# The MoE router reads transposes of the unnormalised residual; the row factor, the scale and the shift are moved out of its path

## Chip, cores and metric

The kernel runs on one core of a Trainium2 chip, in float32 throughout. The metric is the device time of one execution in microseconds (us); the changed kernel is compared with the kernel before on the same chip. Lower is better.

## What is computed

Two decoder layers over a batch of one with 512 tokens of width 1024. Layer 0 mixes tokens with differential attention, layer 1 with multi-head latent attention (MLA). After each mixer comes a hierarchical mixture of experts: a group (of 4) and then 2 of its 8 experts are chosen for each token. Cut to what the change touches, a layer ends like this:

```
x = x + g_m * mixer(...)                      # last product of the mixer: o @ w_o
h = rms_norm(x, norm_ffn) * (1 + sc_f) + sh_f # rows: 1/sqrt(mean(x^2)+eps); columns: gain, scale, shift
g_prob  = softmax(h @ w_group)                # 4 groups
e_logit = (h @ w_router) of the chosen group  # 4 x 8 experts
...top 2 experts, their weights..., w2(silu(h @ w1) * (h @ w3)) for each chosen expert
x = x + g_f * moe
```

The change rests on an identity: with r the row factor, g = norm_ffn * (1 + sc_f) and s = sh_f, `h @ W = r * (x @ (g * W)) + s @ W`.

## The kernel before

Tokens are cut into T = 4 tiles of 128 rows, channels into C = 8 chunks of 128. Every engine has its own instruction stream, written out by hand in the order in which it runs; semaphores (`sem("res")`, `sem("xt")`, ...) are the only ties between them. TensorE is `pe`, VectorE is `dve`, ScalarE is `act`, GpSimd is `pool`; `sp` issues nearly all weight loads. Since channels are laid out as `p*C + c`, a chunk c of a row is every eighth element of it.

The steps around the change, for layer l, with k = 2l + 1 (names, and lines in the profile):

- `project_out(l)` on TensorE: `product(t)` (L792, 32 records of 128x512 for a tile, two halves n of 16) multiplies the mixer's output by `w_o` into the two PSUM banks of tile t. In layer 0 `turn(t)` (L781) transposes the mixer's output first, and ScalarE's `output_turn` (L1343) copies it out.
- `residual(l, t)` on VectorE: for each half, times the gate row (L1761), then added to `X` (L1762). In layer 0 it also does the last conditioning dot products (L1587), which use up the semaphore `ada`.
- `squares` on ScalarE: sum of squares of the row (L1183), square root (L1185). `normalise_x` on VectorE: reciprocal (L1640), then row factor times `X`, read with stride 8 and written in chunk order to `XN` (L1641).
- `transpose_x` on TensorE (L620): 8 transposes of `XN`'s chunks, which read contiguous elements.
- `modulate` on ScalarE and VectorE, four chunks each (L1193, L1650): PSUM times scale plus shift, to `HT`.
- `logits(t)` on TensorE (L800, 16 records): `HT` times the router matrix `WGR`, 40 columns (32 experts and the 4 groups twice). `keep_busy(bank, n)` (L686) are n products (2n records) without use.
- `gate(l)` on VectorE: softmax, choice and ranks, starting with a maximum over all logits (L1817) and ending in `idx` (L1861). ScalarE does its exponential (L1450).
- GpSimd writes each `XN` tile to DRAM (`xn_d`, L2296) and each `X` tile (`kept_d`, L2297), in layer 0 then one more conditioning vector (`mod_d`, L2252, `gate_out`), whose landing it waits for. Then it gathers the rows of the first expert pairs from `xn_d` by `idx` (L2305).
- `experts(l)`: 16 steps, each with two experts (6 MB of weights). `turn_first_pair` (L874) transposes the first gathered rows; L884 and L899 are the products. SyncE loads expert weights (`expert_unit`, L518) into 20 slots; the slots from the fourth expert pair on are asked for only after both first gathers have landed, the two under `HT` after `sem("lg")`, those under `w_o` after the last `product`.

Of the kernel before, what the change touches and what calls it, by code (L numbers as in the profile page):

```python
# [26 lines left out]
ALU = mybir.AluOpType  # L27
# [3 lines left out]
P = 128  # L31
D = 1024
# [172 lines left out]
def build(nc, A, out):  # L205
    stack = ExitStack()
    with stack:
# [43 lines left out]
        CTL = sb("CTL", [1, 1 + TAILS], I32)  # L251
        posi = sb("posi", [P, T], I32)
# [352 lines left out]
        def _(pe):  # L605
# [7 lines left out]

            def transpose_x(k, t):

                if k in (1, 3):
                    pe.wait_ge(sem("res"), 4 * (k // 2) + t + 1)
# [153 lines left out]
            def project_out(l):  # L771
# [13 lines left out]
                def product(t):  # L785
# [4 lines left out]
                    for n in range(2):  # L790
# [6 lines left out]
                def logits(t):  # L797
                    modulated(k1, t)
                    for c in range(C):
                        last = mm(PB[0][:, t * NR:(t + 1) * NR], HT[:, c, t * P:(t + 1) * P], WGR[:, c, :],  # L800
                                  start=c == 0, stop=c == C - 1)
# [361 lines left out]
        def _(act):  # L1163
# [8 lines left out]
            fn(condb, condb, ACT.Silu).then_inc(sem("cond"), 1)  # L1172

            def squares(k, t):
# [10 lines left out]
                fn(sd[:, t:t + 1], ss[:, t:t + 1], ACT.Sqrt, bias=eps, scale=1.0 / D).then_inc(sem("sd"), 1)  # L1185
# [280 lines left out]
            def modulate_first_pair(l):  # L1466

                for h, (turned, done) in enumerate((("xh", "xhA"), ("xgt", "xA"))):
                    act.wait_ge(sem(turned), PAIRS * l + 1 if h else l + 1)
# [79 lines left out]
            output_root(3)  # L1549
            output_turn(2)  # L1550
# [6 lines left out]
            mla()  # L1557
            norm(3)
# [5 lines left out]
        def _(dve):  # L1564
# [49 lines left out]
            def first_block():  # L1614
# [5 lines left out]
                dve.wait_ge(sem("cond"), 1)  # L1620
# [16 lines left out]
            def normalise_x(k, t):  # L1637

                dve.wait_ge(sem("sd"), 4 * k + t + 1)
                link(v.reciprocal(rs[:, t:t + 1], sd[:, t:t + 1]))  # L1640
# [13 lines left out]
            def norm(k, update):  # L1654

                for t in range(T):
                    update((k - 1) // 2, t)
                    normalise_x(k, t)
                    if t:
                        modulate(k, t - 1)  # L1660
                modulate(k, T - 1)
# [90 lines left out]
            def residual(l, t):  # L1752
# [3 lines left out]
                for n in range(2):  # L1756
# [5 lines left out]
                    last = tt(X[:, t, cols], X[:, t, cols], tmp, ALU.add)  # L1762
                    if l == 0 and n == 0:
# [45 lines left out]
            def gate(l):  # L1809

                bgr = bgrs[:, l].rearrange("p (g e) -> p g e", g=NCOL)
                logits = PB[0][:, 0:T * NR].rearrange("p (t g e) -> p t g e", t=T, g=NCOL)
# [3 lines left out]
                dve.wait_ge(sem("lg"), 4 * (l + 1))  # L1816
                link(red(top, logits, AX.X, ALU.max))  # L1817
                tt(scores_, logits, over(top, 3, EPG), ALU.subtract).then_inc(sem("el"), 1)
# [27 lines left out]
                dve.wait_ge(sem("rank"), 2 * l + 1)  # L1846
# [8 lines left out]
                dve.wait_ge(sem("rank"), 2 * l + 2)  # L1855
# [88 lines left out]
            def modulate_first_pair(l):  # L1944

                for h, (turned, done) in enumerate((("xh", "xhD"), ("xgt", "xD"))):
                    dve.wait_ge(sem(turned), PAIRS * l + 1 if h else l + 1)
# [209 lines left out]
            def tables():  # L2157
# [14 lines left out]
                dve.wait_ge(sem("sin"), 1)  # L2172
# [5 lines left out]
                dve.wait_ge(sem("sin"), 2)  # L2178
# [23 lines left out]
            norm(1, residual)  # L2202
            gate(0)
            experts(0)
            gains(2)
            latents()
            mla()
            gains(3)
# [215 lines left out]
```

## Time and profile before

| | us |
|---|---|
| median of 3 runs (1142.84 to 1145.66) | 1144.5 |
| the profiled execution, its own time | 1146.95 |
| its span, first to last instruction | 1145.2 |
| TensorE busy, share of the span | 91% |
| VectorE busy | 53% |
| ScalarE busy | 29% |
| GpSimd busy | 8% |
| DMA, mean over the span | 298 GB/s |

The span is what the views of the trace speak of; 1.75 us of the profiled execution's time lie around it. Busy shares are means over the whole span: whether an engine matters in a stage is read in that stage.

### The profile page before, as it was taken

How to read it: one execution, taken by the hardware profiler on the slowest of the kernel's cores; microseconds unless marked ns; L12 is line 12 of the kernel's file. 1: busy time of each engine (PE TensorE's matmuls, PEld its weight loads, DVE VectorE, ACT ScalarE, POOL GpSimd, SP SyncE). 2: the span in 40 equal slices, each digit the busy share in tenths (PEclk: the TensorE clock that was granted, in tenths of full speed). 3: DMA queues.
4: the chain of work that ended last, by engine and by line, in shares of the span. 5: the costliest groups of instructions: out<-in, count | busy, mean ns of one | idle time of the engine just before them, and what ended most of it. 6: DMA issues, size and time to landing. Idle time of an engine off the chain costs nothing.

```text
span 1145.2 us, 15244 instructions
## 1 busy us (share of the span) xinstructions
PE 1043.2 (91%) x5634; PEld 629.8 (55%) x5634; DVE 608.7 (53%) x1464; ACT 328.3 (29%) x894; POOL 91.7 (8%) x129
## 2 busy tenths in 40 slices
PE   4999999999998999897879999899999999978996
PEld 3444444655566666554536555555457765655652
DVE  6899988895666422121246577677235622212224
ACT  4321122874221112120124554566112112111110
POOL 1000000000011221111000000000000111101100
PEclk9999999999999999999989999999998999999999
DMA  9929868309889999999996201300826799999998
GB/s 367 401 81 414 331 255 331 151 1 382 354 320 372 417 419 419 418 418 420 417 387 260 111 1 38 130 18 33 338 96 268 288 409 418 420 418 411 419 417 358
DMA packets 66814, 341.44 MB, mean 298 GB/s; under 512 B 11110, under 2 KB 11366, under 8 KB 36400
## 3 DMA queue, kind: packets, MB, share of 16 engines
q1 hardware_dynamic: 49952, 297.68, 64.3%
q0 software_dynamic: 15120, 37.63, 8.5%
q10 hardware_dynamic: 1664, 5.09, 1.1%
q8 instruction: 48, 0.79, 0.3%
q14 instruction: 30, 0.25, 0.1%
HBM read 320.90 MB, written 37.24 MB: 313 GB/s over the span
## 4 chain that ended last, share of the span: by engine, by line
PE 73%; DMA 11%; SPq 5%; DVE 5%; ACT 3%; issue 3%; DVEq 0%; ACTq 0%; POOLq 0%
PE PP L884 14%; PE PP L677 12%; PE PP L792 10%; PE PP L899 7%; SPq L518 5%; PE PP L699 3%; DMA AHS<-in_moe_w 3%; PE PP L1050 3%; DMA ring<-in_moe_w 3%; PE PP L1092 3%; PE PP L650 2%; DMA AHS<-y_d 2%; PE PP L1096 2%; PE PP L686 2%; PE PP L857 2%
## 5 line engine op out<-in xcount | busy, mean ns | idle before, releaser
L677 PE MATMUL PP<-ring,AHS 128*128 128x512 f32 x320 | 139.9, 592 | 0.0
L1957 DVE TENSOR_TENSOR PS<-PS,PP 128x256 f32<-128x256 f32 x33 | 13.9, 422 | 196.2 <-PE PP L884 186.6
L792 PE MATMUL PP<-ring,AHS 128*128 128x512 f32 x256 | 111.3, 593 | 1.4 <-ACT AHS L1421 0.8
L1964 DVE SCALAR_TENSOR_TENSOR PS<-PP,small,GF 128x512 f32<-128x512 f32 x66 | 46.5, 747 | 111.8 <-PE PP L899 101.5
L677 PEld LDWEIGHTS PP<-ring,AHS 128*128 128x128 f32 x320 | 59.7, 190 | 69.8 <-issue 69.8
L884 PE MATMUL PP<-RQK,RV 128*64 128x256 f32 x640 | 74.9, 392 | 11.5 <-issue 9.3
L792 PEld LDWEIGHTS PP<-ring,AHS 128*128 128x128 f32 x256 | 48.1, 190 | 59.7 <-issue 59.7
L884 PE MATMUL PP<-ring,RV 128*64 128x256 f32 (+1 forms) x608 | 75.5, 389 | 4.8 <-ACT RV L1455 1.7
L1479 ACT ACTIVATE PS<-PP 128x256 f32<-128x256 f32 x33 | 12.7, 384 | 219.0 <-PE PP L884 164.3
L884 PEld LDWEIGHTS PP<-RQK,RV 128*64 128x64 f32 x640 | 56.0, 141 | 33.3 <-issue 19.8
L884 PE MATMUL PP<-AHS,RV 128*64 128x256 f32 x640 | 71.8, 380 | 1.5 <-issue 1.5
L884 PEld LDWEIGHTS PP<-ring,RV 128*64 128x64 f32 (+1 forms) x608 | 55.6, 144 | 24.6 <-issue 9.0
L884 PEld LDWEIGHTS PP<-AHS,RV 128*64 128x64 f32 x640 | 53.5, 137 | 20.6 <-issue 6.3
L1703 DVE TENSOR_REDUCE small<-PP 128x2 f32<-128x256 f32 (+3 forms) x64 | 52.6, 823 | 16.4 <-PE PP L702 16.2
L2319 POOL DMA_INDIRECT y_d<-PS,row x31 | 31.6, 1020 | 342.5 <-DVE PS L1964 313.9
L1483 ACT ACTIVATE PS<-PP 128x256 f32<-128x256 f32 x33 | 12.7, 384 | 146.8 <-PE PP L891 146.8
L1587 DVE SCALAR_TENSOR_TENSOR ring<-ring,PS 128x1024 f32<-128x1024 f32 x44 | 51.9, 1221 | 3.5 <-DMA ring<-in_ada_t 3.1
L1933 DVE TENSOR_SCALAR RV<-PP,small 128x128 f32<-128x128 f32 x124 | 42.4, 406 | 18.2 <-PE PP L857 18.2
L1455 ACT ACTIVATE RV<-PP,small 128x128 f32<-128x128 f32 x124 | 46.6, 463 | 5.3 <-PE PP L857 5.3
L1281 ACT ACTIVATE AHS<-PP,small 128x512 f32<-128x512 f32 (+3 forms) x80 | 43.9, 558 | 14.3 <-DVE small L1703 14.1
L899 PE MATMUL PP<-AHS,PS 128*64 128x512 f32 (+1 forms) x168 | 40.2, 597 | 7.2 <-ACT PS L1483 6.5
L899 PE MATMUL PP<-ring,PS 128*64 128x512 f32 x160 | 36.5, 597 | 8.3 <-ACT PS L1483 5.4
(346 smaller groups left out, 1679.1 us busy)
## 6 DMA issues: line engine op xcount, KB each, us to landing
AHS<-in_moe_w SPq DMA_DIRECT2D x61, 1024.0 KB, 12.0
ring<-in_moe_w SPq DMA_DIRECT2D x58, 1024.0 KB, 19.1
RQK<-in_moe_w SPq DMA_DIRECT2D x52, 1024.0 KB, 20.4
ring<-in_ada_t SPq DMA_DIRECT2D x22, 1024.0 KB
AHS<-in_ada_t SPq DMA_DIRECT2D x18, 1024.0 KB
X<-in_moe_w SPq DMA_DIRECT2D x16, 1024.0 KB, 23.2
ring<-in_da_w_qkv SPq DMA_DIRECT2D x10, 1024.0 KB, 9.7
RQK<-in_ada_t SPq DMA_DIRECT2D x8, 1024.0 KB, 10.6
```

The costliest lines, as they stand in the source:

```text
L518: sp.dma_start(unit(slot), (w1, w3, w2)[k // 2][l][n + PAIRS * (k % 2)]).then_inc(s_w[slot], 16)
L677: last = mm(PB[qkv_bank(n)][:, :], HT[:, c, t * P:(t + 1) * P], us[c // 4][:, (c % 4) * NH:(c % 4 + 1) * NH], start=c == 0, stop=c == C - 1)
L699: mm(o[:, 0:L], mq[g // 2][0:QK, h, t * P:L], mk[g // 2][0:QK, h, 0:L], start=True, stop=False)
L792: last = mm(PB[2 * t + n][:, :], (OT, OTM)[l][:, k, t * P:(t + 1) * P], us[k // 2][:, (k % 2) * D + n * NH:(k % 2) * D + (n + 1) * NH], st ...
L884: last = mm(o[s0:s1, 0:FF], xgT[b][:, c, s0:s1], w(2 * m + e)[:, c * FF:(c + 1) * FF], start=c == 0, stop=c == C - 1)
L899: last = mm(PB[5 + m][s0:s1, :], hidT[:, c, s0:s1], w(4 + e)[:, c * D + m * NH:c * D + (m + 1) * NH], start=c == 0, stop=c == 1)
L1281: last = fn(dst[:, a, 0:L], PB[2 * pair + a][:, 0:L], ACT.Exp, bias=nmx[:, b, a:a + 1], accum_out=total)
L1455: last = fn(xgT[b][:, c, :], PB[0][:, (c // 2) * P:(c // 2 + 1) * P], ACT.Identity, bias=MODC[:, l, 3 + V_SHIFT, c:c + 1], scale=GC[:, 2 * ...
L1587: last = stt(wt, wt, 1.0, condb, ALU.mult, ALU.mult, accum_out=MODC[:, l, w, 2 * q + c:2 * q + c + 1])
L1703: red(nmx[:, b], PP[pair][:, :, 0:L], AX.X, ALU.max, negate=True).then_inc(sem("nm"), 1)
L1933: last = ts(xgT[b][:, c, :], PB[1][:, (c // 2) * P:(c // 2 + 1) * P], GC[:, 2 * l + 1, c:c + 1], MODC[:, l, 3 + V_SHIFT, c:c + 1], ALU.mul ...
L1964: last = stt(ysb[b][:, cols], PB[5 + m][:, :], weight, GF[:, cols], ALU.mult, ALU.mult)
```

## The change

In both layers TensorE transposes `X` itself, with stride 8, as soon as `residual` is done. What comes out of PSUM is copied without a factor: by ScalarE (chunks 0 to 3) and VectorE (chunks 4 to 7) for tiles 0 to 2, by VectorE alone for tile 3. GpSimd multiplies `WGR` once by the column scale. A product of the shift vector (broadcast) with `WGR`, before that multiplication, gives the same row in each partition, which ScalarE copies to `shifted`. The row factor is `exp(-0.5 ln(.))` on ScalarE instead of a square root and a reciprocal, and is applied to the logits together with `shifted` by `gate`. The normalised rows are still made for `xn_d`, the last tile's now by ScalarE. `product(3)` is cut into its two halves, with `transpose_raw(2)` and `logits(1)` between them and `logits(2)` behind. Compiled, ScalarE's stream has four table loads fewer. VectorE's `gains(3)`, one operation on 8 columns, stands ahead of layer 1's mixer instead of behind it.

```diff
+            def transpose_raw(k, t):
+                pe.wait_ge(sem("res"), 4 * (k // 2) + t + 1)
+                raw = X[:, t, :].rearrange("p (m c) -> p c m", c=C)
+                for c in range(C):
+                    last = nc.tensor.transpose(PB[2 * t + c // 4][:, c % 4 * P:(c % 4 + 1) * P], raw[:, c, :], ident[:, :])
+                    if t == T - 1 and c == C // 2 - 1:
+                        last.then_inc(sem("xh"), 1)
+                last.then_inc(sem("xt"), 1)
...
+                def router_shift():
+                    pe.wait_ge(sem("wgr"), 16 * (l + 1))
+                    pe.wait_ge(sem("gc"), k1 + 4)
+                    for c in range(C):
+                        last = mm(PB[4][:, 0:NR], MODC[:, l, 3 + V_SHIFT, c:c + 1].broadcast_to([P, P]), WGR[:, c, :],
+                                  start=c == 0, stop=c == C - 1)
+                    last.then_inc(sem("rank"), 1)
...
                 turn(1)
+                router_shift()
                 us = [take(l, "wo", u) for u in range(4)]
                 product(0)
+                if l == 0:
+                    pe.wait_ge(sem("wgs"), 2)
                 turn(2)
                 turn(3)
                 product(1)
-                transpose_x(k1, 0)
+                transpose_raw(k1, 0)
                 product(2)
-                transpose_x(k1, 1)
-                pe.wait_ge(sem("wgr"), 16 * (l + 1))
+                transpose_raw(k1, 1)
                 logits(0)
-                product(3)
-                transpose_x(k1, 2)
+                product(3, (0,))
+                transpose_raw(k1, 2)
                 logits(1)
-                keep_busy(3, 7)
-                transpose_x(k1, 3)
+                product(3, (1,))
                 logits(2)
+                keep_busy(3, 2)
+                transpose_raw(k1, 3)
                 logits(3)
...
     # ScalarE
-                fn(sd[:, t:t + 1], ss[:, t:t + 1], ACT.Sqrt, bias=eps, scale=1.0 / D).then_inc(sem("sd"), 1)
+                    chain.link(fn(sd[:, t:t + 1], ss[:, t:t + 1], ACT.Ln, bias=eps, scale=1.0 / D))
+                    fn(rs[:, t:t + 1], sd[:, t:t + 1], ACT.Exp, scale=-0.5).then_inc(sem("sd"), 1)
...
+            def raw_out(k, t):
+                act.wait_ge(sem("xt"), 4 * k + t)
+                fn(HT[:, 0:4, t * P:(t + 1) * P], PB[2 * t][:, :].rearrange("p (c q) -> p c q", c=4), ACT.Identity).then_inc(
+                    sem("hA"), 1)
...
                 squares(k, 0)
-                for t in range(T):
-                    if t + 1 < T:
-                        squares(k, t + 1)
-                    modulate(k, t)
+                squares(k, 1)
+                raw_out(k, 0)
+                squares(k, 2)
+                raw_out(k, 1)
+                raw_out(k, 2)
+                squares(k, 3)
+                act.wait_ge(sem("sd"), 4 * k + T)
+                fn(XN[:, 3, :].rearrange("p (c m) -> p c m", c=C), X[:, 3, :].rearrange("p (m c) -> p c m", c=C), ACT.Identity,
+                   scale=rs[:, 3:4]).then_inc(sem("xn"), 1)
...
     # VectorE
+                residual(l, 0)
+                normalise_x(k, 0)
+                residual(l, 1)
+                raw_out(k, 0, 1)
+                normalise_x(k, 1)
+                residual(l, 2)
+                raw_out(k, 1, 1)
+                normalise_x(k, 2)
+                residual(l, 3, lambda: raw_out(k, 2, 1))
+                raw_out(k, 3, 0)
+                raw_out(k, 3, 1)
...
-                dve.wait_ge(sem("lg"), 4 * (l + 1))
-                link(red(top, logits, AX.X, ALU.max))
+                for t in range(T):
+                    dve.wait_ge(sem("lg"), 4 * l + max(3, t + 1))
+                    last = stt(logits[:, t], PB[t // 3][:, t * NR:(t + 1) * NR], rs[:, t:t + 1], shifted[:, :], ALU.mult, ALU.add)
+                link(last)
+                link(red(top, scores_, AX.X, ALU.max))
...
     # GpSimd, ahead of its wait for the attention's end
+                pool.wait_ge(sem("rank"), 3 * l + 1)
+                g.tensor_tensor(WGR[:, :, :], WGR[:, :, :], GC[:, 2 * l + 1, :].unsqueeze(2).broadcast_to([P, C, NR]),
+                                ALU.mult).then_inc(sem("wgs"), 1)
```

Line numbers of the changed kernel differ: its L812 is the product's L792, L823 is L800, L695 is L686, L1825 and L1826 are L1761 and L1762, L1885 is the new operation of `gate`.

**TensorE, end of the output projection in layer 0**, before, from the second record of `product(3)` to the last logits:

```order
L792 MATMUL PP<-ring,AHS 128x512 x15
L620 MATMUL PP<-ident,RV 128x128 [waits s_xn,s_res]
L620 MATMUL PP<-ident,RV 128x128 x7
L800 MATMUL PP<-WGR,AHS 128x40 [waits s_hD,s_hA]
L800 MATMUL PP<-WGR,AHS 128x40 x7
L686 MATMUL PP<-ident 128x128 x7
L620 MATMUL PP<-ident,RV 128x128 [waits s_xn,s_res]
L620 MATMUL PP<-ident,RV 128x128 x7
L800 MATMUL PP<-WGR,AHS 128x40 [waits s_hD,s_hA]
L800 MATMUL PP<-WGR,AHS 128x40 x7
L800 MATMUL PP<-WGR,AHS 128x40 [waits s_hD,s_hA]
L800 MATMUL PP<-WGR,AHS 128x40 x7
```

and of the changed kernel, from the first logits behind the first half of `product(3)`:

```order
L823 MATMUL PP<-WGR,AHS 128x40 [waits s_hA]
L823 MATMUL PP<-WGR,AHS 128x40 x3
L823 MATMUL PP<-WGR,AHS 128x40 [waits s_hD]
L823 MATMUL PP<-WGR,AHS 128x40 x3
L812 MATMUL PP<-ring,AHS 128x512 [waits s_otev]
L812 MATMUL PP<-ring,AHS 128x512 x7
L823 MATMUL PP<-WGR,AHS 128x40 [waits s_hA]
L823 MATMUL PP<-WGR,AHS 128x40 x3
L823 MATMUL PP<-WGR,AHS 128x40 [waits s_hD]
L823 MATMUL PP<-WGR,AHS 128x40 x3
L695 MATMUL PP<-ident 128x128 x2
L620 MATMUL PP<-ident,X 128x128 [waits s_res]
```

The logits of tile 1 stand ahead of the last half product, those of tile 2 right behind it, and the last tile's transposes come after them and wait for `res`, no more for `xn`.

**VectorE, last half of tile 3 and start of `gate` in layer 0**, before:

```order
L1761 TENSOR_TENSOR PS<-PP,GM 128x512 [waits s_wo]
L1762 TENSOR_TENSOR X<-X,PS 128x512 [waits s_dve]
L1640 RECIPROCAL small<-small 128x1 [waits s_sd,s_res]
L1641 TENSOR_SCALAR RV<-X,small 128x1024 [waits s_dve]
L1650 TENSOR_SCALAR AHS<-PP,small 128x128 [waits s_xt,s_gc]
L1650 TENSOR_SCALAR AHS<-PP,small 128x128 x3
L1650 TENSOR_SCALAR AHS<-PP,small 128x128 [waits s_xt,s_gc]
L1650 TENSOR_SCALAR AHS<-PP,small 128x128 x3
L1817 TENSOR_REDUCE PS<-PP 128x20 [waits s_lg,s_iota,s_kept]
L1818 TENSOR_TENSOR PS<-PP,PS 128x160 [waits s_dve]
```

and of the changed kernel:

```order
L1825 TENSOR_TENSOR PS<-PP,GM 128x512 [waits s_wo]
L1826 TENSOR_TENSOR X<-X,PS 128x512 [waits s_dve]
L1709 COPY AHS<-PP 128x4x128 [waits s_xh,s_res]
L1709 COPY AHS<-PP 128x4x128 [waits s_xt]
L1885 SCALAR_TENSOR_TENSOR PS<-PP,small,shifted 128x40 [waits s_sd,s_lg,s_iota,s_kept]
L1885 SCALAR_TENSOR_TENSOR PS<-PP,small,shifted 128x40 [waits s_lg] x3
L1887 TENSOR_REDUCE PS<-PS 128x20 [waits s_dve]
L1888 TENSOR_TENSOR PS<-PS 128x160 [waits s_dve]
```

Reciprocal, normalisation and the eight scale-and-shift operations behind the last residual are gone; two copies of 128x512 and four small operations on the logits stand in their place.

**GpSimd, from the last tile's two writes to the first gathers in layer 0** of the changed kernel (before, the same rows stand there):

```order
L2369 DMA xn_d<-RV 128x1024 [waits s_xn]
L2370 DMA kept_d<-X 128x1024
L2322 DMA mod_d<-small 128x8 [waits s_mod]
L2378 DMA RV<-xn_d,idx 128x1024 [waits s_xd,s_idx,s_mo,s_res]
L2378 DMA RV<-xn_d,idx 128x1024
```

Nothing moved here; what `s_xn` waits for in the first row is now made by ScalarE, and the first gather waits, besides `idx`, for the landing of `mod_d` (`s_mo`).

## Rows read from the trace of the kernel before

**Rows 1.** Whole execution by core: span, granted clock
```profile
core 0: 1145.2 us, clock 0.984
```

**Rows 2.** Chain that ended last, in time: start us, us, what
```profile
349.75 5.91 DMA RV<-xn_d,idx
...
532.40 31.05 DMA AHS<-in_moe_w
...
1099.03 7.06 PE PP L884 x64
```

**Rows 3.** Timeline, layer 0 tail: start us, us, engine, line, operation [idle <-releaser]
```profile
328.69 1.04 PE L620 MATMUL PP<-ident,RV 128*128 128x128 f32 x8
...
328.89 0.69 DVE L1761 TENSOR_TENSOR PS<-PP,GM 128x512 f32<-128x512 f32 x1 [0.67 <-PE PP L792]
...
329.56 1.88 PE L800 MATMUL PP<-WGR,AHS 128*128 128x40 f32 x16
...
329.62 0.69 DVE L1762 TENSOR_TENSOR X<-X,PS 128x512 f32<-128x512 f32 x1
...
330.34 1.06 ACT L1183 ACTIVATE PS<-X 128x1024 f32<-128x1024 f32 x1 [13.53 <-DVE X L1762]
...
331.27 1.81 PE L686 MATMUL PP<-ident 128*128 128x128 f32 x14
...
331.52 0.30 ACT L1185 ACTIVATE small<-small 128x1 f32<-128x1 f32 x1
...
333.42 1.06 PE L620 MATMUL PP<-ident,RV 128*128 128x128 f32 x8 [0.35 <-DVE RV L1641]
...
334.59 1.50 ACT L1193 ACTIVATE AHS<-PP,small 128x128 f32<-128x128 f32 x4 [1.37 <-PE PP L620]
...
334.70 3.74 PE L800 MATMUL PP<-WGR,AHS 128*128 128x40 f32 x32 [0.21 <-DVE AHS L1650]
...
338.57 0.33 DVE L1817 TENSOR_REDUCE PS<-PP 128x20 f32<-128x160 f32 x1 [2.60 <-PE PP L800]
```

**Rows 4.** Timeline of the same steps in layer 1
```profile
867.47 1.04 PE L620 MATMUL PP<-ident,RV 128*128 128x128 f32 x8
...
873.47 4.54 PE L800 MATMUL PP<-WGR,AHS 128*128 128x40 f32 x32 [0.21 <-DVE AHS L1650]
...
878.15 0.33 DVE L1817 TENSOR_REDUCE PS<-PP 128x20 f32<-128x160 f32 x1 [3.41 <-PE PP L800]
```

**Rows 5.** Windows, one stretch of layer 1 (PEclk is third from the end)
```profile
873.00:878.00 5.00, 4.79 (x35) 4.44 (x33) 1.69 (x6) 2.79 (x5) 0.40 (x1) 0.82 1.00 371
```

**Rows 6.** Timeline where each output projection starts, both layers
```profile
265.91 1.91 PE L781 MATMUL PP<-ident,AHS 128*128 128x128 f32 x16
...
268.39 13.97 PE L792 MATMUL PP<-ring,AHS 128*128 128x512 f32 x32 [0.57 <-ACT AHS L1343]
...
805.77 2.38 PE L747 MATMUL PP<-AHS,RV 128*64 128x512 f32 x16 [0.83 <-ACT AHS L1297]
...
808.92 27.70 PE L792 MATMUL PP<-ring,AHS 128*128 128x512 f32 x64 [0.78 <-ACT AHS L1421]
```

**Rows 7.** Timeline, rows that price reads and copies
```profile
16.91 2.18 ACT L1225 ACTIVATE RV<-X,small 128x1024 f32<-128x1024 f32 x1 [3.27 <-DVE small L1623]
...
332.12 1.16 DVE L1641 TENSOR_SCALAR RV<-X,small 128x1024 f32<-128x1024 f32 x1
...
804.98 0.69 DVE L2135 COPY AHS<-PP 128x512 f32<-128x512 f32 x1 [1.25 <-PE PP L736]
```

**Rows 8.** Timeline, GpSimd's queue in layer 0
```profile
334.69 0.55 POOL L2252 DMA_DIRECT2D mod_d<-small  x1
...
349.75 1.10 POOL L2305 DMA_INDIRECT RV<-xn_d,idx  x1 [14.52 <-DVE idx L1861]
```

**Rows 9.** DMA issues, layer 0 stretch: KB each, us to landing
```profile
mod_d<-small POOLq DMA_DIRECT2D x1, 4.0 KB, 13.1
```

**Rows 10.** DMA issues, layer 1's first gather, us to landing
```profile
RV<-xn_d,idx POOLq DMA_INDIRECT x1, 4.2
```

More of the change, by code:

```diff
@@ L251, in build @@
         CTL = sb("CTL", [1, 1 + TAILS], I32)
+        shifted = sb("shifted", [P, NR])
         posi = sb("posi", [P, T], I32)
@@ L783, in turn, with product @@
                     last.then_inc(sem("ott"), 1)
-                def product(t):
+                def router_shift():
[5 more added lines that the diff above has]
+                    last.then_inc(sem("rank"), 1)
+                def product(t, halves=range(2)):
                     if l == 0:
@@ L789, in product @@
                         pe.wait_ge(sem("omla"), 8)
-                    for n in range(2):
+                    if t == 2:
+                        pe.wait_ge(sem("wgs"), 2 * (l + 1))
+                    for n in halves:
                         for k in range(C):
@@ L1199, in norm, with router_shift @@
                 squares(k, 0)
-                for t in range(T):
-                    if t + 1 < T:
-                        squares(k, t + 1)
-                    modulate(k, t)
+                squares(k, 1)
[7 more added lines that the diff above has]
+                   scale=rs[:, 3:4]).then_inc(sem("xn"), 1)
+            def router_shift(l):
+                act.wait_ge(sem("rank"), 3 * l + 1)
+                fn(shifted[:, :], PB[4][:, 0:NR], ACT.Identity).then_inc(sem("wgs"), 1)
             def root(out_, in_, scale, s):
@@ L1549, in _ @@
             output_root(3)
+            router_shift(0)
             output_turn(2)
@@ L1557, in _ @@
             mla()
+            router_shift(1)
             norm(3)
@@ L1652, in modulate, with raw_out, norm @@
                 last.then_inc(sem("hD"), 1)
[L1654 to L1661, printed above, removed]
+            def raw_out(k, t, half):
+                if half:
+                    dve.wait_ge(sem("xt"), 4 * k + t)
+                else:
+                    dve.wait_ge(sem("xh"), k)
+                v.tensor_copy(HT[:, 4 * half:4 * half + 4, t * P:(t + 1) * P],
+                              PB[2 * t + half][:, :].rearrange("p (c q) -> p c q", c=4)).then_inc(sem("hD" if half else "hA"), 1)
+            def norm(k):
+                l = k // 2
+                residual(l, 0)
[9 more added lines that the diff above has]
+                raw_out(k, 3, 1)
             def da_project():
@@ L1750, in output_norm, with residual @@
                     output_scaled(T - 1, half)
-            def residual(l, t):
+            def residual(l, t, between=lambda: None):
                 if l:
@@ L1762, in residual @@
                     last = tt(X[:, t, cols], X[:, t, cols], tmp, ALU.add)
+                    if n == 0:
+                        between()
                     if l == 0 and n == 0:
@@ L1811, in gate @@
                 bgr = bgrs[:, l].rearrange("p (g e) -> p g e", g=NCOL)
-                logits = PB[0][:, 0:T * NR].rearrange("p (t g e) -> p t g e", t=T, g=NCOL)
+                logits = scores_.rearrange("p t g e -> p t (g e)")
                 slots = picked.rearrange("p t k e -> p (t k) e")
@@ L1815, in gate @@
                 dve.wait_ge(sem("iota"), 2 * l + 1)
-                dve.wait_ge(sem("lg"), 4 * (l + 1))
-                link(red(top, logits, AX.X, ALU.max))
-                tt(scores_, logits, over(top, 3, EPG), ALU.subtract).then_inc(sem("el"), 1)
+                dve.wait_ge(sem("sd"), 4 * (2 * l + 1) + T)
+                for t in range(T):
[3 more added lines that the diff above has]
+                link(red(top, scores_, AX.X, ALU.max))
+                tt(scores_, scores_, over(top, 3, EPG), ALU.subtract).then_inc(sem("el"), 1)
                 dve.wait_ge(sem("ele"), l + 1)
@@ L2201, in _ @@
             dve.wait_ge(sem("gm"), 16)
-            norm(1, residual)
+            norm(1)
             gate(0)
@@ L2205, in _ @@
             gains(2)
+            gains(3)
             latents()
             mla()
-            gains(3)
             dve.wait_ge(sem("gm"), 32)
-            norm(3, residual)
+            norm(3)
             gate(1)
```

31 lines of the change are left out of this document (18 added, 13 removed).

## Prediction

> **What bounds the kernel now.** Start with the whole execution: one core, 1145.2 us of span, TensorE's granted clock at 0.984 [rows 1], so the clock is near its upper level but for short stretches. Then the chain that ended last, in order of time. Its long pieces are TensorE products and, in layer 0's experts, a weight load that TensorE waits 31 us of chain for; in layer 1's experts the pieces are TensorE products to the end (1099.03); in layer 0 the first gather (349.75, 5.91 us) links router and experts [rows 2]. Two consequences. In layer 0 the stream of expert weights decides the end, but it is resumed only when both first gathers have landed, so time gained or lost up to them is still passed on whole. In layer 1 the products decide, which start behind the same gather. I therefore read, in both layers, the stretch from the last product of the output projection to the gather.
>
> Let T0 be the moment at which TensorE starts what follows its last product half: 328.69 in layer 0, 867.47 in layer 1 [rows 3, 4]. The timeline behind it shows one long hand-over: residual to 330.31, squares, root, normalisation, transposes at 333.42, scaling, logits 334.70, and the router's first VectorE operation at 338.57. That is T0 + 9.88 in layer 0 [rows 3] and T0 + 10.68 in layer 1 [rows 4]; the 0.8 more is the logits' 32 records taking 4.54 instead of 3.74 us, in a stretch with a mean granted clock of 0.82, between the levels of 1.2 and 2.4 GHz [rows 5]. The operations from there to `idx` are the same before and after.
>
> **The change, part by part.** I first price everything as if a stride cost nothing.
>
> Ahead of T0, TensorE gets work. Sixteen logits records take 331.27 - 329.56 = 1.71 us, 0.107 each; eight transposes 0.87 [rows 3]. `router_shift` is 16 such records, 1.71. It partly fills idle time: in layer 0 sixteen transposes from 265.91 at 0.109 end at 267.65, and the first product starts at 268.39, so 0.74 is covered; in layer 1, 805.77 + 2.38 to 808.92 covers 0.77 [rows 6]. It costs 0.97 and 0.94. The transposes of tile 2 and the logits of tile 1 move from behind the last half product to ahead of it: 0.87 + 1.71 = 2.58. So T0 comes 3.55 and 3.52 later.
>
> Behind the new T0: logits of tile 2, 1.71; four `keep_busy` records at about 0.11, 0.45; transposes start at 2.16. `res` comes at 1.62 (329.62 + 0.69 - 328.69) and isn't waited for. Four transposes take 0.44. The first reader of eight transposes starts 1.17 after them, 0.30 beyond their 0.87 [rows 3]; so the first copy starts at 2.9. VectorE's PSUM copy of 128x512 takes 0.69 [rows 7]: 3.59, the second copy by 4.3. A signal costs 0.14 (end of the normalisation, 333.28, to 333.42). The first half of the logits runs 3.73 to 4.58, the second, no longer waiting, to 5.44. From the logits' last issue to VectorE it is 0.45 (334.70 + 32 x 0.107 to 338.57) [rows 3]: 5.9. The last of four 128x40 operations has no row; nothing bounds it below, the 0.33 of the 128x160 reduction above; I take 0.2 and get 6.1. The other three lie behind the logits. The tail is 3.8 shorter in layer 0 and 4.6 in layer 1. Net on `idx`: -0.2 and -1.1, the second mostly the clock, which may dip again.
>
> What costs nothing: ScalarE's and VectorE's copies for tiles 0 to 2, each with a product half of 6.9 us beside it; the table loads that are gone, which lay beside the residual's waits and the logits; GpSimd's 128x320 product, with product(0)'s 14 us before anyone waits for it. That last one stands ahead of GpSimd's zero fill of `y_d` in layer 0 and delays it, and the row writes behind it, by a few us; the gather that needs them leaves some 80 us later, at 349.75 [rows 8]. If this cover were gone, TensorE would wait for `wgs` ahead of `turn(2)`.
>
> **Stride.** The raw transposes read every eighth float, 32 bytes apart. No row shows TensorE doing so. Two other engines do, on the same `X`: ScalarE takes 2.18 us for 1024 elements [rows 7], against 1.06 for 1024 contiguous ones [rows 3], 2.06 times. VectorE takes 1.16 [rows 7], 0.145 per 128 elements with its fixed part. Bounds for one transpose: 0.109 (nothing), 0.145 (VectorE's pace), 0.22 (twice), 0.27 (ScalarE's pace). TensorE's present pace, 128 elements in 0.109, is 1.17 elements per ns, faster than ScalarE's contiguous pace of 0.97 and than VectorE's strided 0.88, so it is nearer to the engine that halves. I take 0.22, +0.11 each. Three tiles lie ahead of T0: 24 x 0.11 = 2.6. Behind it the first copy starts 0.44 later, the second waits for all eight (2.16 + 1.76 + 0.3 = 4.2, to 4.9), the second half of the logits starts at 5.03 instead of 4.58: +0.5. Together +3.1 per layer; `idx` moves by +2.9 and +2.0.
>
> The Trainium skill, "SBUF — State Buffer", section "Door 1: The DMA port swizzle", says that SBUF is read in lines of 16 bytes and that fp32 can be strided freely up to four elements; beyond that each access opens a new line and pays. By it stride 8 costs TensorE something and the sum is the +3.1 per layer; by VectorE's row, which shows hardly any price, it would be 28 x 0.036 = 1.0. ScalarE's 2.18 us agrees with the page, VectorE's 1.16 doesn't show it.
>
> **GpSimd's queue in layer 0.** The last tile's rows are now normalised by ScalarE: residual 1.62, squares to root 1.18 (330.34 to 331.52), logarithm and exponential at 0.30 each, like the root [rows 3], 2.18 for the strided read [rows 7], signals 0.2: ready at T0' + 5.8. Before, `mod_d` was issued at 334.69, 1.41 behind the end of the normalisation at 333.28, and took 13.1 us to land, at 347.8, behind 1 MB of rows and beside the weights [rows 8, 9]. GpSimd waits for it ahead of the first gather, which left at 349.75, released by `idx` [rows 8]: 2 us of margin. After, it is issued at T0' + 7.2, so at 328.69 + 3.55 + 7.2 = 339.4 without a stride price and 342.1 with it, and lands at 352.5 or 355.2. The gather then leaves 2.8 or 5.4 later than before, not with `idx`. In return fewer weights are beside it: layer 1's took 4.2 us [rows 10], layer 0's 5.91 [rows 2], so up to 1.7 comes back. Layer 0: between +2.9 (`idx` alone) and +5.4; I take +4. In layer 1 there is no `mod_d`; the writes of the rows have over 10 us.
>
> **Sum.** 4 + 2.0 = +6. The profiled execution would go from 1146.95 to 1153; it stands 2.45 above the median of the runs, 1144.5, so I forecast 1150.5.
>
> **Rivals.**
> - *The stride is free or nearly so for TensorE.* For it: VectorE's 1.16 us. Against it: ScalarE's row. Then `idx` comes 0.2 and 1.1 earlier; with `mod_d` late layer 0 gives +1 to +2.8: together about +0.7, 1145.2; with `mod_d` in time, -1.3, 1143.2. Not slower. It decides up to where 56 transposes' worth of extra cost makes 3.4 us with `mod_d` late: below 0.16 to 0.17 us a transpose.
> - *The stride costs, `mod_d` doesn't.* Its 13.1 us were spent beside the weight stream; issued later it may meet a shorter queue. Layer 0 then gives +2.9: total +4.9, 1149.4.
> - *TensorE reads at ScalarE's pace*, 0.27: another 0.05 x 28 x 2 = 2.8, 1153.
> - *Clearly faster.* Needs 3.4 us: the clock staying high through the router and the first products in both layers, beyond the 0.8 seen. Nothing in the rows gives as much; -4, 1140.5.
>
> **How the numbers follow.** 0.3% is about what a measurement of this kernel can tell from no change, 3.4 us. Stride doubled: 0.52, of which two thirds with `mod_d` late (the forecast), one third without. Nearly free: 0.36. ScalarE's pace or worse: 0.06. Clearly faster: 0.06. The doubled case's own range is 1148 to 1153; the free one's 1142.8 to 1146.5. Both together need 1143 to 1153.5. Slower: 0.52 x 0.9 + 0.06, with a little of the free case, 0.54; faster 0.06; same 0.40.
>
> **What would show it.** The pitch of the eight raw transposes (0.11 or 0.22) in the timeline; T0 at about 335 and 873.6; the router's first 128x160 reduction 6 to 7 us behind it; GpSimd's first gather in layer 0 released by the `mod_d` landing, later than 352; in layer 1 by `idx`. The prediction is wrong if the transposes keep 0.11, or if ScalarE's and VectorE's copies for tiles 0 to 2 make TensorE wait inside the projection.

## The result, and the profile after

The changed kernel took 1150.11 us (median of 7 runs, 1147.17 to 1152.87) where the kernel before took 1144.5 beside it (1142.78 to 1145.92): ratio 1.0038, 95% interval 1.0020 to 1.0056. A second set of runs, taken with the experiments, gave 1149.49 against 1146.54 over 35 runs of before, 1.0021 (1.0004 to 1.0038). These ratios are not the quotients of the medians, which are 1.0049 and 1.0026. So it is slower, by 2.4 to 4.4 us by the two ratios and by 3.0 to 5.6 us by the medians. The forecast was 1150.5.

The span answers to [rows 1]; this execution's own time was 1152.87, the longest of its seven.

```profile
core 0: 1151.0 us, clock 0.987
```

The timeline of layer 0 after the change, where the projection starts, answers to [rows 6]: start us, us, engine, line.

```profile
267.01 1.91 PE L790 MATMUL PP<-ident,AHS 128*128 128x128 f32 x16
...
268.76 1.88 PE L799 MATMUL PP<-WGR,small 128*128 128x40 f32 x16
...
270.46 1.96 PE L812 MATMUL PP<-ring,AHS 128*128 128x512 f32 x4
...
270.72 0.72 POOL L2352 TENSOR_TENSOR WGR<-WGR,small 128x320 f32<-128x320 f32 x1 [77.69 <-PE PP L799]
```

And its tail, which answers to [rows 3]:

```profile
333.46 1.88 PE L823 MATMUL PP<-WGR,AHS 128*128 128x40 f32 x16
...
334.38 0.69 DVE L1826 TENSOR_TENSOR X<-X,PS 128x512 f32<-128x512 f32 x1
...
335.69 1.04 PE L620 MATMUL PP<-ident,X 128*128 128x128 f32 x8
...
336.86 2.15 ACT L1243 ACTIVATE RV<-X,small 128x1024 f32<-128x1024 f32 x1
...
337.14 1.98 PE L823 MATMUL PP<-WGR,AHS 128*128 128x40 f32 x16 [0.41 <-DVE AHS L1709]
...
339.16 0.26 DVE L1885 SCALAR_TENSOR_TENSOR PS<-PP,small,shifted 128x40 f32<-128x40 f32 x1 [0.97 <-PE PP L823]
...
339.45 0.32 DVE L1887 TENSOR_REDUCE PS<-PS 128x20 f32<-128x160 f32 x1
```

Eight raw transposes take 1.04 us, as eight contiguous ones did [rows 3]. T0 is 333.46, and the reduction (339.45) stands 5.99 us behind it, where it stood 9.88 behind. GpSimd's queue in layer 0 answers to [rows 8, 9]; the last row is the view of DMA issues, with KB and us to landing.

```profile
340.41 0.55 POOL L2322 DMA_DIRECT2D mod_d<-small  x1
...
354.09 1.10 POOL L2378 DMA_INDIRECT RV<-xn_d,idx  x1 [13.13 <-DMA mod_d<-small]
...
mod_d<-small POOLq DMA_DIRECT2D x1, 4.0 KB, 12.8
```

`idx` was written at 349.49, so the gather waits 4 us for `mod_d` alone. Layer 1's tail answers to [rows 4]:

```profile
877.39 1.88 PE L823 MATMUL PP<-WGR,AHS 128*128 128x40 f32 x16
...
879.62 1.04 PE L620 MATMUL PP<-ident,X 128*128 128x128 f32 x8
...
883.38 0.32 DVE L1887 TENSOR_REDUCE PS<-PS 128x20 f32<-128x160 f32 x1
```

One pair of profiles is not enough to place a few us, so the table counts each stage from its own start, for all kernels timed here. A0 is the start of the 16 transposes of layer 0's attention output, A1 that of the 16 last value products of layer 1's attention, before as in [rows 6]; E is TensorE's first expert product, X the end of layer 0's last expert product, RQK SyncE's first load of expert weights into the buffer RQK. Each number is the difference of two starts in the timeline or the chain. The kernels below the changed one are those of the experiments.

| kernel | A0 | A0 to RQK | A0 to gather | A0 to E | A0 to X | X to A1 | A1 to gather | A1 to E | E to end |
|---|---|---|---|---|---|---|---|---|---|
| before | 265.9 | 62.20 | 83.84 | 91.55 | 301.3 | 238.6 | 83.48 | 91.06 | 248.4 |
| before_again | 266.5 | 62.20 | 84.70 | 91.40 | 301.4 | 241.8 | 83.47 | 89.58 | 250.0 |
| before_mod_late | 266.3 | 62.20 | 84.69 | 92.21 | 301.5 | 241.4 | 83.47 | 89.53 | 248.9 |
| before_early_ada | 265.5 | 56.91 | 83.81 | 91.25 | 300.2 | 240.3 | 82.60 | 90.18 | 248.8 |
| changed | 267.0 | 63.80 | 87.08 | 93.18 | 303.7 | 241.4 | 82.36 | 89.39 | 249.6 |
| after_again | 266.8 | 63.80 | 87.24 | 93.45 | 303.7 | 238.3 | 82.38 | 89.38 | 249.9 |
| mod_late | 266.9 | 63.80 | 83.52 | 92.82 | 302.5 | 238.4 | 82.37 | 89.35 | 249.7 |
| after_early_ada | 266.5 | 56.58 | 87.33 | 93.46 | 303.7 | 241.4 | 82.36 | 89.30 | 250.2 |
| two_gates | 265.9 | 56.57 | 83.54 | 92.00 | 300.7 | 237.0 | 82.35 | 89.93 | 248.1 |
| tail_order | 266.5 | 63.21 | 84.55 | 92.42 | 302.2 | 239.0 | 82.03 | 88.10 | 251.3 |
| both | 266.7 | 63.21 | 82.41 | 92.50 | 302.4 | 238.5 | 82.20 | 88.21 | 249.8 |
| all_three | 266.6 | 62.30 | 81.49 | 91.33 | 301.7 | 236.8 | 81.29 | 87.33 | 249.3 |
| all_four | 266.4 | 55.70 | 81.50 | 89.02 | 298.1 | 241.5 | 80.35 | 86.38 | 250.0 |

The end is that of the span. Three things are to be read here. X to A1, which the change hardly touches, varies from 236.8 to 241.8 in kernels of all kinds: of the 5.8 us between the two first spans, 2.8 are this, and no effect of the change. What the change does repeatedly is A0 to X, +2.3 us, and A1 to the gather, -1.1. The 1.1 us don't reach the experts: layer 1's first gather takes 5.2 us to land where it took 4.2 [rows 10], so it lands only 0.1 to 0.2 us earlier against A1 (87.5 to 87.6 in place of 87.7 to 87.8). From A1 to the end the first four kernels of the table need 338.4 to 339.6 us, the changed one 339.0 and 339.3. Here is the view of DMA issues, and the 5 us from just before this gather on (columns of the windows: GpSimd busy, PEclk, DMA share, GB/s), before and after:

```profile
RV<-xn_d,idx POOLq DMA_INDIRECT x1, 5.2
...
889.00:894.00 5.00, 2.08 (x2) 0.66 0.43 116
...
894.00:899.00 5.00, 2.08 (x2) 1.00 0.92 375
```

In the changed kernel the gather meets expert weights that are still under way: SyncE's loads behind the last product leave 3.7 us later against A1 (877.59 in place of 867.66). In tail_order and the kernels built on it the last product ends earlier again, and this gather lands 4.2 to 4.3 us after its issue.

### The profile page after: what moved, and what is told of

It reads as the page before. It is cut to its first block, busy times and chain, and to the rows that moved or that the text cites. A ratio compares the mean times of both kernels' runs of the same rounds, so it can differ in the third digit from the quotient of the medians.

```text
span 1151.0 us, 15203 instructions
## 1 busy us (share of the span) xinstructions
PE 1042.2 (91%) x5646; PEld 630.0 (55%) x5646; DVE 602.6 (52%) x1440; ACT 321.1 (28%) x876; POOL 93.7 (8%) x131
## 4 chain that ended last, share of the span: by engine, by line
PE 70%; DMA 14%; SPq 6%; DVE 4%; ACT 3%; issue 3%; POOL 0%; DVEq 0%; ACTq 0%; POOLq 0%
PE PP L910 13%; PE PP L686 12%; PE PP L812 10%; PE PP L925 7%; SPq L519 6%; DMA ring<-in_moe_w 5%; PE PP L708 3%; PE PP L1076 3%; DMA AHS<-in_moe_w 3%; PE PP L1118 3%; PE PP L659 2%; DMA AHS<-y_d 2%; PE PP L1122 2%; PE PP L745 2%; PE PP L756 2%
## 5 line engine op out<-in xcount | busy, mean ns | idle before, releaser
L686 PE MATMUL PP<-ring,AHS 128*128 128x512 f32 x320 | 139.9, 592 | 0.0
L812 PE MATMUL PP<-ring,AHS 128*128 128x512 f32 x256 | 111.8, 594 | 0.0
L686 PEld LDWEIGHTS PP<-ring,AHS 128*128 128x128 f32 x320 | 59.7, 190 | 69.8 <-issue 69.8
L812 PEld LDWEIGHTS PP<-ring,AHS 128*128 128x128 f32 x256 | 48.0, 190 | 56.9 <-issue 56.9
L1825 DVE TENSOR_TENSOR PS<-PP,GM 128x512 f32<-128x512 f32 x16 | 11.1, 692 | 65.0 <-PE PP L812 65.0
```

The lines of the kernel that those rows point to most:

```text
L686: last = mm(PB[qkv_bank(n)][:, :], HT[:, c, t * P:(t + 1) * P], us[c // 4][:, (c % 4) * NH:(c % 4 + 1) * NH], start=c == 0, stop=c == C - 1)
L812: last = mm(PB[2 * t + n][:, :], (OT, OTM)[l][:, k, t * P:(t + 1) * P], us[k // 2][:, (k % 2) * D + n * NH:(k % 2) * D + (n + 1) * NH], st ...
```

## Experiments

**after_again.** The changed kernel once more, beside the three edits that follow.

> The changed kernel, unchanged, timed again and profiled again. In the first trace the first gather of layer 0 leaves 4.3 us late, released by the landing of mod_d; between the layers another 2.5 us are lost in a stretch where four products take 3.6 instead of 1.9 us. Queue theory: the late gather is there again (GpSimd's first gather of layer 0 released by mod_d, 2.7 to 3.5 us of the expert phase), so at least 0.2% slower than before. Clock theory for the rest: the loss between the layers is TensorE's clock falling by chance and will be larger or smaller this time, so the ratio lies between 1.001 and 1.006. Stride theory (the prediction's): raw transposes at 0.22 us; the first trace already shows 0.109 and this one should again.

1149.49 us (1146.63 to 1152.55), ratio 1.0021 (1.0004 to 1.0038). Its stages agree with the first profile's to 0.3 us but for X to A1, which is 3.1 shorter.

**mod_late.** `mod_d` is written behind the first two gathers.

```diff
-                if l == 0:
-                    gate_out(1, 1)
                 pool.wait_ge(sem("res"), T * (l + 1))
...
                 for n in range(2):
                     gather_pair(n)
+                if l == 0:
+                    gate_out(1, 1)
```

> The changed kernel with one move: GpSimd issues the mod_d write of layer 0, and waits for its landing, behind the first two gathers instead of ahead of them. Queue theory: the first gather leaves as soon as idx is there, about 0.8 us after it, at some 350.5 instead of 354.1; the gathers then run beside the last weights (5.9 instead of 4.3 us), so the expert phase starts 2 to 3 us earlier and the time falls by 2 to 3 us against the changed kernel, to 0.1 to 0.2% above before. If instead the delay of the expert phase comes from the residual, the copies or the transposes, nothing moves: 0.4% slower than before, as the changed kernel.

1148.56 us, ratio 1.0007 (0.9991 to 1.0023). The timeline of GpSimd, and the chain behind the gather:

```profile
350.44 1.08 POOL L2376 DMA_INDIRECT RV<-xn_d,idx  x1 [10.09 <-DVE idx L1931]
...
352.86 0.60 POOL L2322 DMA_DIRECT2D mod_d<-small  x1
...
350.44 7.49 DMA RV<-xn_d,idx
```

The gather is now released by `idx`, 3.6 to 3.7 us earlier against A0, but it takes 7.49 us to land in place of 4.30 and 4.41, and E comes only 0.4 to 0.6 us earlier. The 2 to 3 us that were expected didn't come. The release was not the only thing that held it.

**tail_order.** The last product isn't split round tile 2's transposes any more.

```diff
-                product(3, (0,))
+                product(3)
                 transpose_raw(k1, 2)
                 logits(1)
-                product(3, (1,))
-                logits(2)
-                keep_busy(3, 2)
+                pe.wait_ge(sem("hA"), 4 * k1 + 3)
                 transpose_raw(k1, 3)
+                logits(2)
                 logits(3)
...
-                residual(l, 3, lambda: raw_out(k, 2, 1))
+                residual(l, 3)
+                raw_out(k, 2, 1)
```

> The changed kernel with another order at the end of the output projection: both halves of the last product first, then the raw transposes of tile 2, logits of tile 1, raw transposes of tile 3, logits of tiles 2 and 3, without keep_busy. TensorE has 6.9 us of such work behind the last product and the last tile's hand-over needs about 5.4, so work moved ahead of the last product is paid in full beyond 1.5 us. Theory of the moved work: the router's reduction comes 1.1 us earlier in each layer than in the changed kernel (about 7.5 us behind the last product against 2.6 + 6.0), and the row writes and mod_d of layer 0 are issued 2.6 us earlier, which is what its gather waits for: together -2.6 and -1.1, about 3.7 us below the changed kernel. If the moved work were hidden in waits as it was, no change or slower by the 0.5 us that the copies then lie open.

1146.41 us, ratio 0.9995 (0.9979 to 1.0012), 3.1 us below after_again by the medians, where 3.7 were expected. `idx` comes 1.1 us earlier in layer 0 (A0 + 81.35 in place of 82.48), but only 0.3 us earlier in layer 1 (A1 + 81.04 in place of 81.38); A1 to E is 1.3 us shorter all the same, because the gather lands sooner.

**both**: `mod_late` and `tail_order` together.

> mod_late and tail_order together. Queue and moved-work theories: against before, idx comes 1.4 us earlier in layer 0 (0.97 for the shift's product, 7.5 instead of 9.9 us behind the last product) and 2 us in layer 1: 1141 us, 0.3% faster than before, if nothing else in the change costs time. Seen from the changed kernel, the two edits are worth 5.5 us, which would give 1144.6, no change against before: the 3 us between these two are what neither theory explains (clock between the layers, or something in the change that the first trace does not show). This run tells which.

1145.72 us, ratio 0.9992 (0.9978 to 1.0007). Layer 0's gather leaves at A0 + 82.41, 1.1 us ahead of mod_late's, yet it takes 8.3 us to land and E gains only 0.3. The time is 1.1 us over the higher of the two sums that were expected, 1144.6.

**stride_probe.** The kernel before, with 16 raw transposes in place of its seven dummy products (`keep_busy`, 14 records).

```diff
-                keep_busy(3, 7)
+                strided(16)
...
+                def strided(n):
+                    raw = X[:, 0, :].rearrange("p (m c) -> p c m", c=C)
+                    for j in range(n):
+                        nc.tensor.transpose(PB[3][:, 0:P], raw[:, j % C, :], ident[:, :])
```

> The kernel before, in which the dummy matmuls between tile 3's product and its normalized transposes give place to 16 transposes of tile 0's X in the layout of the changed kernel (8 elements between one operand column and the next), written to a bank that nobody reads, once in each layer; the output is the reference's. My prediction's price: 0.22 us a transpose, so the 16 take 3.5 us in place of 1.75 and the reduction over the logits comes 1 us or more later than in the kernel before (338.57 and 878.15 us). The rival, that the stride costs nothing at a full clock: 0.109 us each, 1.75 us for 16, reduction within 0.3 us of before.

A single run, 1147.43 us, so only its trace is read here. TensorE's timeline:

```profile
331.15 2.02 PE L800 MATMUL PP<-ident,X 128*128 128x128 f32 x16
...
333.34 1.07 PE L620 MATMUL PP<-ident,RV 128*128 128x128 f32 x8 [0.17 <-DVE RV L1646]
```

Sixteen end 0.98 us later than eight would (1.04), 0.12 each, where 0.22 each would have made 3.5 us; the reduction stands at 338.49 and 878.38, within 0.25 of before. The stride is free for TensorE's pace. The view of one line's instructions shows where it went, first of the changed kernel and then of before:

```profile
L620 PEld LDWEIGHTS PP<-ident,X x64: 185/188/193, 299.3 to 880.3; 128*128 128x128 f32 x64
```

```profile
L620 PEld LDWEIGHTS PP<-ident,RV x96: 138/140/144, 297.3 to 872.9; 128*128 128x128 f32 x96
```

The numbers are minimum, median and maximum in ns. With the stride the transposes' weight load grew from 140 to 188, while their matmuls have a median of 273 in both kernels. I read this as the strided operand being the one that is loaded as weights; the load lies beside the matmul ahead of it. How much of the 48 ns is a price of the stride isn't settled: the loads of ordinary products, which read contiguous elements, take 190 in the kernel before (L792), at the same pace.

**before_again.** The kernel before once more, for its own spread.

> The kernel before, unchanged: a second profile and its own spread. In the five profiles of changed kernels TensorE's second product (at 39.61 to 39.93 us) begins 0.8 to 1.1 us later than in the one profile of before (38.83), since its first matmuls run slower for a little longer, and this offset then stays until the attention's end. If that is chance, this profile shows some start between 38.8 and 40.0; if the change does it, 38.8 again. The time: ratio 1.000 within 0.0015.

1146.47 us, ratio 0.9987 (0.9972 to 1.0002). The chain has its first 16 matmuls of the opening projection at 7.18 us and the next at 31.68, where the first profile had 6.87 and 31.09 and the changed kernel 7.49 and 32.19. It lies between them: TensorE's slower start is at least partly chance. A0 is 265.5 to 266.5 in the kernels of before, 265.9 to 267.0 in those with the change; whether the 0.6 us between their means belongs to the change stays open.

**before_mod_late.** The same move of `mod_d` in the kernel before.

> The kernel before with GpSimd's write of mod_d moved behind the first two gathers of layer 0, as in mod_late. If a gather's landing is held by the backlog of weight loads that SyncE issued (the landing came 27.2 to 27.6 us after the first of them, RQK, was issued, in before, mod_late and both alike), nothing changes: gather released by idx at 349.7, landed at 355.7, time 1.000 within 0.0015. If mod_d's 4 KB and its small packets themselves hold up the queue, the gather lands earlier than 355.2 and the kernel is up to 0.5 us faster.

1146.62 us, ratio 0.9998 (0.9980 to 1.0016). Nothing changes, as the theory of the weight backlog had it: released by `idx`, the gather lands at A0 + 90.0, before at 89.75 and 89.6. The rival, that `mod_d`'s small packets hold it up, would have had it earlier.

**all_three**: both, and the shift row's matmuls in two halves where TensorE waits.

```diff
+                router_shift(0, 0)
                 da_values(31)
...
+                router_shift(1, 0)
                 for k in range(T):
                     mla_values(7, k)
...
-                router_shift()
+                router_shift(l, 1)
```

In layer 1 the row goes to a bank that is free at that time.

> The version called both, and the shift row's 16 matmuls in two halves put where TensorE waits (before the last value product and ahead of the first output product). The shift cost 0.97 and 1.13 us on the path; placed so some 0.3 each should be left, so the first weight load for the experts (RQK) is issued 0.7 us earlier than in both (329.86), the layer 0 gather lands 0.7 us earlier (356.7) if the backlog theory holds, and layer 1 gains 0.8. Sum 1.3 to 1.5 us faster than both: about 1144.3 where both had 1145.7, ratio to before 0.9975 to 0.9985. If the waits of TensorE in the attention are not free time (a late product behind them), ratio as both, 0.9992.

1144.41 us, ratio 0.9981 (0.9965 to 0.9997). The first product starts 2.55 and 3.21 us after A0 and A1, in place of 3.45 and 4.11 (before 2.48 and 3.15), so of the shift's cost nearly all is gone. Against both, RQK is issued 0.9 us earlier and E comes 1.2 and 0.9 us earlier.

**before_early_ada, after_early_ada, all_four.** RQK is free for expert weights only when VectorE has done the last two products with the modulation's weights (`ada`), and it does them behind the first half of tile 3's residual. This is SyncE's queue before and after the change, and the DMA share of 325 to 330 us (columns of the windows: VectorE busy, PEclk, DMA share, GB/s), before:

```profile
328.11 0.81 SPq L518 DMA_DIRECT2D RQK<-in_moe_w  x2
...
325.00:330.00 5.00, 4.26 (x9) 1.00 0.15 28
```

after:

```profile
324.12 0.69 DVE L1825 TENSOR_TENSOR PS<-PP,GM 128x512 f32<-128x512 f32 x1 [5.20 <-PE PP L812]
...
329.49 1.22 DVE L1635 SCALAR_TENSOR_TENSOR RQK<-RQK,PS 128x1024 f32<-128x1024 f32 x1
...
330.81 0.81 SPq L519 DMA_DIRECT2D RQK<-in_moe_w  x2
...
325.00:330.00 5.00, 5.00 (x9) 1.00 0.00 0
```

VectorE waits 5.20 us for the product and then does four dots, one every 1.15 us, while the DMA engines are idle. The edit, the same in all three (all_four is all_three with it):

```diff
                 if l:
                     dve.wait_ge(sem(f"xl{t}"), loaded["mla", t])
+                else:
+                    ada(LATE + 2 * t)
+                    ada(LATE + 2 * t + 1)
                 for n in range(2):
...
-                    if l == 0 and n == 0:
-                        ada(LATE + 2 * t)
-                        ada(LATE + 2 * t + 1)
```

> The kernel before, in which VectorE does the last eight ada units' dots in layer 0 ahead of its wait for each output product instead of behind that product's first half. Theory (weight backlog): layer 0's experts are bound by weight loads that start when VectorE frees RQK after the last two dots; in all nine profiles the experts' last product ends 238.7 to 239.9 us after SyncE issues the first of these loads, and the first gather lands 27.2 to 27.9 us after it. DMA idles 5.4 us of 320 to 335 in before. So RQK's load should be issued 3 to 6 us earlier than 328.1 and the experts end 2 to 5 us earlier after the attention's end: ratio 0.9960 to 0.9985. Rival (TensorE and the gather's own chain bound it): the load is earlier but the experts' start (91.4 to 92.2 us after the attention's end) and end stay, ratio 0.9990 to 1.0010. If the dots wait for their units and hold up the residual, T0 later and 1.001 to 1.003.

1145.63 us, ratio 0.9996 (0.9981 to 1.0012). RQK is issued 5.3 us earlier, X comes 1.1 us earlier, the time stays; 0.9960 to 0.9985 was expected. One reason stands in its trace: the gather lands at A0 + 88.19, but TensorE is in its 44 dummy records until the turn at A0 + 89.54.

> The changed kernel with the same move of the dots. By the backlog theory the changed kernel lost 1.6 us in layer 0 only because RQK's load came 1.6 us later against the attention's end (63.80 us in place of 62.20), and DMA idled some 9 us of 320 to 335 in it: the load 5 to 8 us earlier, the first gather still issued when mod_d landed (354.1), landing at 356 to 358.3, experts' end 3 to 6 us earlier, ratio to before 0.9970 to 0.9990 where the changed kernel had 1.0021. By the rival 1.002 as it was.

1148.17 us, ratio 1.0021 (1.0004 to 1.0038): no gain. The gather still leaves when `mod_d` has landed (A0 + 87.33), E and X stand where they stood. My theory that the loads alone set the end of the experts is refuted by this run.

> The version all_three with the same move of the dots; gather released by idx at about 348. By the backlog theory RQK's load 3 to 6 us earlier than 328.9, experts' end in layer 0 2 to 5 us earlier; time 1140 to 1142.5, ratio 0.9945 to 0.9965 where all_three had 0.9981. By the rival 0.998.

1142.05 us (1140.53 to 1144.27), ratio 0.9956 (0.9941 to 0.9972; the quotient of the medians is 0.9968). SyncE and the gather:

```profile
322.10 0.80 SPq L519 DMA_DIRECT2D RQK<-in_moe_w  x2
...
347.90 1.08 POOL L2379 DMA_INDIRECT RV<-xn_d,idx  x1 [11.64 <-DVE idx L1934]
...
325.00:330.00 5.00, 0.51 (x1) 1.00 0.75 315
```

With the gather released early, the same move is worth 2.3 us at E and 3.5 at X, though here too the turn waits 1.4 us for the dummies (landing at 352.32, turn at 353.72). This version beats both kernels.

**two_gates.** The changed kernel with mod_late and the early dots, nothing else.

> The changed kernel with both edits and nothing else: mod_d's write behind the first two gathers (mod_late) and the ada dots ahead of the residual's waits (after_early_ada). From the attention's end to the experts' first matmul of layer 0 the changed kernel needs 93.2 and 93.5 us, with the first edit alone 92.8, with the second alone 93.5, before 91.4 to 92.2. Theory (two gates on one gather, mod_d on its release and the weight backlog on its landing, each hiding the other): with both gone the gather is released by idx some 83.5 us after the attention's end and the experts begin 7.4 to 7.6 us after that, as in before_early_ada and all_four: 90.9 to 91.1 us, 2.2 to 2.5 us less than the changed kernel; ratio to before about 1.000 where the changed kernel had 1.0021. Rival (the two edits add up as they stood alone): 92.8 us and 1.0015.

1145.68 us, ratio 0.9997 (0.9981 to 1.0013). E comes at A0 + 92.00, between the theory's 91.0 and the rival's 92.8; at X the two together give 2.9 us, where they gave 1.1 and 0.0 alone, so they hide one another. The miss has a row: the gather, issued at 349.48, landed 5.5 us later at 354.95, but TensorE was still in its dummies, as in before_early_ada and all_four.

```profile
348.65 7.75 PE L695 MATMUL PP<-ident 128*128 128x128 f32 x44 [0.56 <-DVE idx L1931]
...
356.24 1.04 PE L900 MATMUL PP<-ident,RV 128*128 128x128 f32 x8
```

They lie in a stretch (350 to 358 us) with a mean granted clock of 0.75, so part of it ran at the lower of the two levels. That fewer dummies would let the turn start at the landing was not tried.

## Why the prediction came out as it did

The time was right to 0.4 us, by luck: the step that carried most of it was wrong. Without the stride's price the forecast's own sum is +0.7 us and not +6. What stood in its place, in the first runs, was +2.3 us in layer 0, nothing in layer 1 where -1.1 was due, perhaps 0.6 us at the start, and spread; the second set of runs is 3.0 us above the kernel before, by the medians.

- **Stride: failed.** "I take 0.22, +0.11 each", +3.1 us per layer. Measured: 0.11 each in the changed kernel's own rows, 0.12 in stride_probe, so next to nothing. I took ScalarE's pace because TensorE's was nearest to it in elements per ns. But I compared with TensorE's matmuls, and the strided reads are in its weight loads, which have a track of their own beside the matmuls and grew from 140 to 188 ns without moving them.
- The Trainium skill, "SBUF — State Buffer", section "Door 1: The DMA port swizzle", lets an access that crosses into a new 16-byte line pay. The weight load's 48 ns more agree with it in kind, as far as they are the stride's (contiguous loads of ordinary products take 190 too). The kernel's pace, 0.11 to 0.12 us a transpose, shows no price, so the page's rule was no ground for a term of the sum.
- **Ahead of T0: right.** The shift cost 0.97 and 0.96 (3.45 - 2.48, 4.11 - 3.15; predicted 0.97 and 0.94). The moved transposes and logits cost 2.70 and 2.69 (first product to T0 63.00 and 61.24, less 60.30 and 58.55), predicted 2.58.
- **Tail: right without the stride.** 5.99 in both layers, predicted 6.1, and 0.5 more with the stride's price.
- **`idx` if the stride is free: right.** -0.2 and -1.1 predicted; -0.2 (82.70 to 82.48) and -1.1 (82.49 to 81.38) measured in the first pair. The kernel before needs 83.6 in layer 0 in before_again and before_mod_late, 0.63 to 0.95 more of it between T0 and the reduction, so layer 0's gain on `idx` is 0.2 to 1.2 by the profile one compares with. In layer 1 the gain is real at `idx` and at the gather's release, and is lost in its landing, as shown below the table.
- **GpSimd's queue in layer 0: right in the trace, mis-sized in worth.** I forecast a gather released by `mod_d` later than 352, and it left at 354.09. I had the landing as its release plus 4 to 6 us. In fact a second gate stood at the same place: the expert weights, whose first load moved from A0 + 62.20 to A0 + 63.80, because the dots that free their buffer stand on VectorE behind the later residual (0.97, the shift) and the new copy (0.68). tail_order, which moves the copy away, has 63.21, and all_three, which hides most of the shift too, 62.30. The first gather landed 27.2 to 27.9 us after this load in before, changed, mod_late, tail_order, both and all_three, whether it had been issued 4.3 us ahead of its landing (changed) or 8.3 (both). The prediction named no such queue; it is SyncE's.
- The Trainium skill, "DMA: Bandwidth & Descriptors", section "Issuing engines are not separate DMA queues", says that transfers of all engines run on the same 16 engines and interleave. Our traces agree: the first gather, on GpSimd's queue, took 7.49 us in mod_late beside SyncE's loads and 5.5 in two_gates, 8.04 in all_three and 4.4 in all_four, that is less once the first of those loads had been issued earlier.
- **Layer 0 as a whole**: +4 forecast, +2.3 measured at X. **Layer 1**: +2.0 forecast; -1.1 at the gather's release, -0.1 to -0.2 at its landing, and no gain at the end that these profiles can tell. The forecast passed a gain up to the gather on whole, and that step failed here too.
- That makes +2.1 to +2.3, or up to +2.9 with the open 0.6 us of the start, where the two comparisons say 2.3 to 6.4 and 0.5 to 4.4 us by their intervals. The rival "the stride is free", with `mod_d` late, said +0.7 and had the mechanism but for the weight backlog; the time came out nearer to the forecast. The rest is not placed stage by stage: parts that the change doesn't touch vary by up to 5 us (X to A1), and this is as large as the effect.

## What to carry to other kernels

Price an access pattern on the unit that reads it: here the strided operand went through the weight load, which had slack, and a row of another engine misled by 3.1 us a layer. When a wait is removed and the time stays, ask what else ends at that moment and remove both: `mod_d`'s landing and the weight backlog hid one another, alone 1.1 and 0.0 us, together 2.9. Read a gain where the data lands and not where the transfer is issued: layer 1's 1.1 us were gone by then. Work that frees a buffer for a prefetch (the dots on RQK) belongs ahead of a wait and not behind it, above all where the DMA engines are idle meanwhile.

## What was unexpected of the hardware

- A 4 KB write issued behind 1 MB of row writes, beside weight loads, took 12.8 to 13.4 us to land; behind the gathers it took 5.5 (mod_late) and 6.4 (both, all_three), and 3.0 to 3.6 in all_four, two_gates and before_mod_late.
- TensorE's weight load of 128x128 fp32 with a stride of 8 elements took 188 ns against 140 in a transpose, with no change of its matmuls' pace (a contiguous load for an ordinary product took 190); ScalarE's 1024 such elements took 2.15 us in the same kernel.
- The first 16 matmuls of the opening projection took 6.87 to 7.63 us, with a granted clock of 1.00 in the windows of this stretch, and the later start (1.1 us between the first two profiles) stays to the end of layer 0's attention.
